# One layer-stack kernel, seven edits to its order: the start, the third output slabs, the last microseconds

## The reference

```
h = rmsnorm(x, g) * (1 + scale) + shift
x = x + gate * mixer(h)                     # layer 0: gated delta rule, 8 heads; layer 1: latent attention
h = rmsnorm(x, g') * (1 + scale') + shift'
x = x + gate' * swiglu(h)                   # width 2816
```

## Time and profile before

| | |
|---|---|
| median of three executions | 2261.05 us (2259.95 to 2262.13) |
| the profiled execution | 2260.28 us, its span 2258.4 us |
| busy: PE, DVE, ACT, POOL | 2163.2, 1168.5, 581.9, 1217.0 us |
| DMA | 240.40 MB, 106 GB/s over the span |

### The profile page before, as it was taken

The page is one execution under the profiler, slowest core; times in us unless marked ns, Lnnn a source line. Parts: engine busy times, 40 slices in busy tenths (PEclk is TensorE's granted clock), DMA queues, the critical chain, the costliest instruction groups (busy, mean ns, idle before and its releaser), DMA issues.

```text
span 2258.4 us, 29283 instructions
## 1 busy us (share of the span) xinstructions
PE 2163.2 (96%) x11996; PEld 1727.1 (76%) x11996; DVE 1168.5 (52%) x1634; ACT 581.9 (26%) x1054; POOL 1217.0 (54%) x688
## 2 busy tenths in 40 slices
PE   5999999899999999998999999999999999999997
PEld 4777777778888887676788888777767878887886
DVE  3566666657648275554431322467755365346332
ACT  4432433213102022342320201422332230002113
POOL 4532233347868776432566666654445276657663
PEclk9999999999999999999999999999999999999999
DMA  9422222226556463211433333322214133333331
GB/s 304 142 67 85 88 81 85 85 70 210 178 171 206 141 195 110 68 51 30 120 94 96 100 94 99 97 75 75 66 52 126 38 112 96 100 85 93 103 103 66
DMA packets 366016, 240.40 MB, mean 106 GB/s; under 512 B 11350, under 2 KB 350524, under 8 KB 365756
## 3 DMA queue, kind: packets, MB, share of 16 engines
q1 hardware_dynamic: 364268, 234.60, 34.5%
q10 hardware_dynamic: 1616, 3.93, 0.5%
HBM read 234.31 MB, written 4.19 MB: 106 GB/s over the span
## 4 chain that ended last, share of the span: by engine, by line
PE 88%; DVE 6%; POOL 2%; issue 2%; ACT 2%; DMA 1%; SPq 0%; ACTq 0%; DVEq 0%; POOLq 0%
PE bank L588 16%; PE bank L590 16%; PE bank L589 16%; PE bank L607 6%; PE bank L609 5%; PE bank L608 5%; PE mid L871 2%; PE mid L1333 1%; POOL wL L544 1%; PE bank L624 1%; DMA stage<-in_c_wkv 1%; PE bank L625 1%; PE bank L626 1%; PE mid L632 1%; PE bank L825 1%
## 5 line engine op out<-in xcount | busy, mean ns | idle before, releaser
L542 POOL TENSOR_SCALAR wH<-stage 128x1024 fp32r<-128x1024 f32 (+1 forms) x340 | 386.6, 1137 | 985.7 <-PE bank L609 375.1
L544 POOL TENSOR_TENSOR wL<-stage,wH 128x1024 fp32r<-128x1024 f32 (+1 forms) x340 | 830.3, 2442 | 28.4
L588 PE MATMUL bank<-hH,wH 128*128 128x512 f32 x944 | 368.7, 391 | 0.7 <-DVE A L2051 0.3
L590 PE MATMUL bank<-hH,wL 128*128 128x512 f32 x944 | 367.4, 389 | 0.0
L589 PE MATMUL bank<-hL,wH 128*128 128x512 f32 x944 | 367.3, 389 | 0.0
L588 PE MATMUL bank<-RA,wH 128*128 128x512 f32 (+1 forms) x788 | 285.8, 363 | 15.1 <-POOL wL L544 12.1
L590 PE MATMUL bank<-RA,wL 128*128 128x512 f32 (+1 forms) x788 | 282.7, 359 | 0.0
L589 PE MATMUL bank<-RA,wH 128*128 128x512 f32 (+1 forms) x788 | 282.7, 359 | 0.0
L607 PE MATMUL bank<-hH,wH 128*128 128x512 f32 x544 | 238.6, 439 | 0.3 <-DVE A L2051 0.3
L609 PE MATMUL bank<-hH,wL 128*128 128x512 f32 x544 | 213.5, 393 | 0.0
L608 PE MATMUL bank<-hL,wH 128*128 128x512 f32 x544 | 213.2, 392 | 0.0
(11 more groups left out here) (390 smaller groups left out, 3244.1 us busy)
## 6 DMA issues: line engine op xcount, KB each, us to landing
WIDE<-in_ada_t SPq DMA_DIRECT2D x48, 1024.0 KB, 6.1
stage<-in_ffn_w_gate SPq DMA_DIRECT2D x44, 512.0 KB, 3.9
stage<-in_ffn_w_up SPq DMA_DIRECT2D x44, 512.0 KB, 3.9
stage<-in_c_wkv SPq DMA_DIRECT2D x32, 512.0 KB, 3.9
stage<-in_gdn_w_in SPq DMA_DIRECT2D x32, 512.0 KB, 4.1
stage<-in_ffn_w_down SPq DMA_DIRECT2D x32, 512.0 KB, 3.8
stage<-in_o_w_in SPq DMA_DIRECT2D x32, 512.0 KB, 4.0
stage<-in_e_w_in SPq DMA_DIRECT2D x26, 512.0 KB, 3.8
```

The costliest lines, as they stand in the source:

```text
L542: pool.tensor_scalar(high[:, 0:n], raw[:, 0:n], 1.0, 0.0, ALU.mult, ALU.add).then_inc(w_high, 1)
L544: pool.tensor_tensor(low[:, 0:n], raw[:, 0:n], high[:, 0:n].bitcast(F32), ALU.subtract).then_inc(w_split, 1)
L588: pe.matmul(bank[:, 0:n], h[:, k, c], xh[:, k, :], start=first and k == 0, stop=False)
L590: mm = pe.matmul(bank[:, 0:n], l[:, k, c], xh[:, k, :], start=False, stop=last and k == kc - 1)
```

## The change

- **Start, loads.** x is loaded ahead of the memory; only the first two tables are loaded first, the rest and the column constants after the first two head slabs; kv slabs and groups alternate in SP's queue; a third slot holds groups; groups come in the order 0, 4, 1, 5, 2, 6, 3, 7, so that two of them complete two chunks' shift and scale; group 7 is loaded behind two head slabs; the small parameters come behind the seventh group.
- **Start, c.** c is loaded as one row by ACT's queue, and TensorE spreads it over the partitions with two multiplications by ones.
- **Start, x.** x is turned before the memory and copied by DVE instead of ACT. The memory turns have four banks instead of two.
- **Start, norm.** The norm is done two chunks at a time, in DVE's queue between the groups (`first_norm`), and in ACT's between the copies of kv slabs (`first_high`).
- **Gates.** The high and the low part of the 16 gate columns lie side by side, so two multiplications a chunk give all; the sums are added on DVE.
- **Third slabs divided.** Two to four thirds stand ahead of the last step, the others behind it, at all six places; in gdn five stand in the last head's later fillings and three behind.
- **End.** The squares' sums are taken in two halves, the last chunk's turned copy is DVE's, ACT's table is loaded ahead of the residual, and row blocks are sent in the order 2, 0, 3, 1.

```diff
+ADA_ORDER = (0, 4, 1, 5, 2, 6, 3, 7)
...
+        adaw.append(A[:, 12:16].rearrange("p (r a) t -> p r (a t)", r=ADA_ROWS))
...
+                slot = ada_use(n)[0]
+                if n >= 3:
+                    sp.wait_ge(ada_summed, n - 2 if n < ADA_HEAD else n - 1)
...
-            sp.dma_start(tab[:], a["square"]).then_inc(small_in, 16)
-            sp.dma_start(cols2[:], a["cols"]).then_inc(small_in, 16)
+            sp.dma_start(tab[:, 0:2 * P], a["square"][:, 0:2 * P]).then_inc(small_in, 16)
...
+            load_kv(2)
+            load_ada(1)
+            load_kv(3)
+            sp.wait_ge(m["mem"], 1)
             load_ada(2)
+            load_kv(4)
+            load_ada(3)
...
+            head_slabs(0, range(2))
+            load_ada(7)
+            sp.dma_start(tab[:, 2 * P:], a["square"][:, 2 * P:]).then_inc(tab_in, 16)
+            sp.dma_start(cols2[:], a["cols"]).then_inc(tab_in, 16)
+            head_slabs(0, range(2, 4))
...
-            for t in range(TT):
+            for t in (2, 0, 3, 1):
                 sp.wait_ge(scaled_out[t], 1)
...
+            pe.wait_ge(c_in, 17)
+            for n in range(2):
+                mm = pe.matmul(c_bank[:, n * T:(n + 1) * T], ones[0:1, :], cbc[0:1, n * T:(n + 1) * T], start=True, stop=True)
...
+            x_turn(range(KD))
+            for n in range(4):
+                memory(0, n)
             pe.wait_ge(x_memt, 8)
-            kv_slabs("m0", range(2))
...
+            kv_slabs("m0", (0,))
             norm_squares(range(4))
-            kv_slabs("m0", (4,))
+            kv_slabs("m0", (1,))
             norm_squares(range(4, KD))
-            kv_slabs("m0", range(5, 8))
+            kv_slabs("m0", range(2, 8))
...
-                pe.matmul(B3[:], h, hH[:, k, :], start=k == 0, stop=False)
-                pe.matmul(B3[:], h, hL[:, k, :], start=False, stop=False)
-                mm = pe.matmul(B3[:], l, hH[:, k, :], start=False, stop=k == KD - 1)
+                both = RA[:, 0, 32 * k:32 * k + P]
+                pe.matmul(B3[:], both, hH[:, k, :], start=k == 0, stop=False)
+                mm = pe.matmul(B3[:], both, hL[:, k, :], start=False, stop=k == KD - 1)
...
-                    fill(24 + t, 25 + t, third=(t,))
+                    fill(24 + t, 25 + t)
...
-                fill(28, 30, third=(4, 5))
+                fill(28, 30, third=(0, 1))
...
-                fill(30, 32, 6, third=(6,))
+                fill(30, 32, 6, third=(2, 3, 4))
...
-            out_third("gdn_out", 7, 7, 8)
+            for k in range(5, KD):
+                out_third("gdn_out", k, k, k + 1)
...
-            for k in range(2, 6):
-                out_third("mla_out", k, k, 8 + k + 1)
+            out_third("mla_out", 2, 2, 8 + 3)
             for k in (6, 7):
                 out_step("mla_out", k, k, 8 + k + 1)
-            for k in (6, 7):
+            for k in range(3, KD):
                 out_third("mla_out", k, k, 8 + k + 1)
...
-            for n in range(7):
+            for n in range(4):
                 e_out(n, out_third)
             e_out(7)
-            e_out(7, out_third)
+            for n in range(4, KD):
+                e_out(n, out_third)
...
-                for k in range(6):
+                for k in range(2):
                     out_third(f"x{r}_out", k, k, 24 + 16 * r + k + 1)
...
-                for k in (6, 7):
+                for k in range(2, KD):
                     out_third(f"x{r}_out", k, k, 24 + 16 * r + k + 1)
...
-            for k in range(KD - 1):
+            for k in range(2):
                 out_third("o_out", k, k, 32 + k + 1)
             out_step("o_out", KD - 1, KD - 1, 32 + KD)
-            out_third("o_out", KD - 1, KD - 1, 32 + KD)
+            for k in range(2, KD):
+                out_third("o_out", k, k, 32 + k + 1)
...
+            early_copies((0,))
             squares_of_x(range(4))
+            early_copies((1,))
             squares_of_x(range(4, KD))
+            inv_sqrt(ss_done, SS0[1], SS, SS[:], 1.0 / D, load=False).then_inc(rstd_ready, 1)
+            early_copies(range(2, 5))
+            first_high(range(2))
             early_copies((5,))
-            rstd_of(RUN_OF["mix0"], SS)
-            early_copies((6, 7))
-            early_spill(1)
-            norm("mix0", modT[:, 0:8], load=False)
+            first_high(range(2, 4))
+            early_copies((6,))
+            first_high(range(4, 6))
+            early_copies((7,))
+            first_high(range(6, KD))
...
+            def first_norm(pair):
+
+                ks = range(2 * pair, 2 * pair + 2)
+                cols = slice(2 * pair, 2 * pair + 2)
+                dve.wait_ge(ada_summed, 2 * pair + 2)
+                own(dve.scalar_tensor_tensor(out=gainA[:, 0, cols], in0=modT[:, 8 + 2 * pair:10 + 2 * pair], scalar=1.0,
+                                             in1=col["mix0"][:, cols], op0=ALU.add, op1=ALU.mult))
+                own.settle()
+                for k in ks:
...
+            for n in range(4):
+                ada_sum(n)
+            dve.wait_ge(x_ready, KD)
+            dve.wait_ge(rstd_ready, 1)
+            for pair in range(2):
+                first_norm(pair)
+            for pair in range(2, 4):
+                for n in range(2 * pair, 2 * pair + 2):
+                    ada_sum(n)
+                first_norm(pair)
```

More of the change, by code:

```diff
@@ L288, in build @@
         taken = [sem(f"taken{n}") for n in range(2)]
-        ada_loaded = [sem(f"ada_loaded{n}") for n in range(2)]
+        ada_loaded = [sem(f"ada_loaded{n}") for n in range(3)]
         ada_summed, c_in = sem("ada_summed"), sem("c_in")
+        tab_in = sem("tab_in")
         small_in, x_in, vec_in, par_in, wide_in, mem_in = (
@@ L725, in _ @@
             pe.wait_ge(vec_ready, 1)
-            for n in range(4):
-                memory(0, n)
+            pe.wait_ge(c_in, 17)
+            for n in range(2):
+                mm = pe.matmul(c_bank[:, n * T:(n + 1) * T], ones[0:1, :], cbc[0:1, n * T:(n + 1) * T], start=True, stop=True)
+            mm.then_inc(m["c"], 1)
             xtok = A[:, 0:8].rearrange("p (t a) c -> p t (a c)", t=TT)
@@ L1497, in memory_rows @@
                     own.settle()
-                own(inv_sqrt(act_own, own.now(), mss[:, 2:4], mss[:, 0:2], 1.0 / D))
+                own(inv_sqrt(act_own, own.now(), mss[:, 2:4], mss[:, 0:2], 1.0 / D, load=r == 1))
                 own.settle()
@@ L2120, in _ @@
             dve.tensor_copy(vec[:, 0:VEC_ROWS], B3[:, 0:VEC_ROWS]).then_inc(vec_ready, 1)
-            dve.wait_ge(m["c"], 1)
-            dve.wait_ge(vec_ready, 1)
-            own(dve.memset(gate_row.bitcast(F32), 0.0))
-            dve.wait_ge(small_in, 32)
+            for k in range(KD):
+                dve.wait_ge(turned, k + 2)
+                dve.tensor_copy(xT[:, k, :], x_banks[k % 2]).then_inc(x_ready, 1)
+            dve.wait_ge(vec_ready, 1)
+            for n in range(4):
+                memory_low(0, n)
@@ new lines, in _ @@
+            own(dve.memset(gate_row.bitcast(F32), 0.0))
+            dve.wait_ge(m["c"], 1)
+            def first_norm(pair):
[5 more added lines that the diff above has]
+                own.settle()
+                for k in ks:
+                    if pair:
+                        dve.wait_ge(h_ready, k - 1)
+                    dve.scalar_tensor_tensor(out=(B4, B7)[k % 2][:], in0=xT[:, k, :], scalar=gainA[:, 0, k:k + 1], in1=SS,
+                                             op0=ALU.mult, op1=ALU.mult).then_inc(t_ready, 1)
+                for k in ks:
+                    dve.wait_ge(hh_ready, k + 1)
+                    dve.scalar_tensor_tensor(out=hL[:, k, :], in0=(B4, B7)[k % 2][:], scalar=modT[:, k:k + 1],
+                                             in1=hH[:, k, :].bitcast(F32), op0=ALU.add, op1=ALU.subtract).then_inc(h_ready, 1)
@@ L2125, in _ @@
+            for n in range(4):
+                ada_sum(n)
[7 more added lines that the diff above has]
+                first_norm(pair)
+            dve.wait_ge(tab_in, 32)
             unit = table("ident64")[0:64]
             dve.tensor_tensor(pick[0:64, :], unit[:, 0:8], unit[:, 32:40], ALU.add).then_inc(g["pick"], 1)
-            ada_sum(0)
@@ L2128, in _ @@
-            for n in range(4):
-                memory_low(0, n)
-            for n in range(1, ADA_HEAD):
-                ada_sum(n)
-            gain_of(0, col["mix0"], 8)
-            dve.wait_ge(x_ready, KD)
-            norm("mix0", gainA[:, 0], modT[:, 0:8])
+            own(dve.tensor_copy(cbc[:], c_bank))
+            dve.wait_ge(h_ready, KD)
             pads = A[:, 14:18].rearrange("p a c -> p (a c)")[:, 0:3 * 516].rearrange("p (n c) -> p n c", n=3)
```

172 lines of the change are left out of this document (88 added, 84 removed).

## The result

The changed kernel takes 2232.82 us (median of four, 2231.63 to 2234.73), the kernel before 2260.50 (four, 2259.64 to 2262.13): a ratio of 0.9876, interval 0.9864 to 0.9888. The span fell from 2258.4 to 2231.0, 27.4 us, where 15.3 were forecast. The direction and most of the single terms were right; one term was much too small and two places were missing from the sum.

What follows compares the result with a forecast made beforehand. TensorE was taken as the bound (88% of the span). Start 1.5, thirds 12.4 and tail 1.4 sum to 15.3 us: 2260.28 - 15.3 = 2245.0, for the median 2245.7; range 2238 to 2252.

Steps and rivals of the forecast that it cites:

- The thirds: Dividing third slabs at six places fills TensorE's waits for GpSimd's split: 12.4 us, of which gdn 1.5.
- The start: The stretch up to TensorE's end of the first eight chunks: 3.9 us earlier, less 2.4 for slow clock, 1.5 us.
- x and the memory land: Loads at the start: memory lands some 2 us later, at 14.2, with bytes priced at 404 GB/s.
- product 0: First weight product on TensorE at the start: 5.5 us, from 24.9 to 30.4.
- the gain that GpSimd blocked: VectorE's gains in the first norm: one of them held up under GpSimd's subtraction, 1.7 us.
- The last low part: End of VectorE's chain in the first norm: 75.9, with TensorE through the eight chunks at 77.1.
- the start is warm: Rival, chance 0.25: turns and c's row bring 2.4 GHz, product 0 takes 2.9, up to 3.7 us earlier, 2242.0.
- the idle time ahead of chunk 6: At the start TensorE waits for chunks and idles about 5 us before chunk 6.
- cost there what they cost here: Small packets of the convolution weights move behind group 6 in the DMA queue, at unchanged cost.
- The loss to the clock: After idling at the start, TensorE's multiplications run at 1.2 GHz, 0.43 apart instead of 0.23: 2.4 us lost.
- The tail: End of the kernel: table load moved ahead and row blocks reordered, first output DMA 1.4 us earlier.

Runs made afterwards that it cites:

- e1: The kernel before with only the six divisions of the third slabs added; 2248.76 us, ratio 0.9942.
- e10: Changed kernel with early high parts, small loads behind two head slabs, and the last head's four-column copy on ScalarE instead of VectorE; 2230.76 us.
- e3: The changed kernel with the thirds of gdn alone put back as before; 2234.48 us, ratio 0.9881.
- e9: The changed kernel with c loaded into all partitions and its silu copied by ScalarE, as before, instead of multiplications by ones; 2235.00 us.
- e8: The changed kernel with 24 unused turns of the identity on TensorE in the hole ahead of the first weight product; 2233.43 us.
- e5: The kernel before with one added wait: GpSimd splits the first gdn_out slab only after VectorE's fourth instruction of the last head; 2257.55 us, ratio 0.9984.

## Why the prediction was wrong, step by step

- **The thirds: right.** Sum 12.4, measured 13.0 alone in e1. The spacing in the earlier trace rows and the hole plus clock in the earlier trace rows carried over to four other places within 0.3 us. In gdn it was 1.7 with the old start (e1) and 1.3 to 1.6 with the new one where the clock held (e10 against e3); in the changed kernel the clock, fallen behind a wait of 1.87, took it back.
- **The start: the failed step, "the start brings 3.9 - 2.4 = 1.5 us"; it brought 5.5 to 7.8.** Three terms of the sum were mis-sized, all the same way: x and the memory land 1.8 us earlier than reckoned (I priced all bytes at 404 GB/s; c's load, which no longer stands ahead of x, had cost 2.4 us and not 1.3 (e9), and the other 0.7 stays open); product 0 took 4.4 and not 5.5, because the turns had brought the clock up (e8, e9); the gain that GpSimd blocked lost 0.7 and not the 1.7 that I took. The last low part came at 70.2 instead of 75.9. These three make 3.9 of the 5.7 us; of the others, 0.7 lies between the scaled memory and product 0, where the memory turns ran at full pace, and 1.0 in the rest of VectorE's chain. The rival "the start is warm", held at 0.25, had the right mechanism, and product 0 gained 1.1 of the 2.6 us that it gave; against it I had held that turns don't lift the clock, which e9 refutes.
- **A wait missed.** The prediction put the idle time ahead of chunk 6. It stood ahead of chunk 0, since the head slab's load had moved behind the small packets. I counted what those cost ("cost there what they cost here") and not who stands behind them in SP's queue. So VectorE's chain ended 5.7 us earlier than forecast, but the chunks only 2.4 (74.7 against 77.1). The loss to the clock is in the 74.7 already (eleven multiplications at 0.43 instead of 0.23, 2.2 us), where the prediction took 2.4 off once more: 2.4 + 2.4 are the 4.8 of the table. That the loss to the clock had nearly the forecast size is luck: it fell behind another hole than the one it was reckoned for.
- **The last head: missing from the sum.** I saw the copy of 2.35 in the earlier trace rows and used it only as a price for the gains at the start. It and its neighbour each waited for one of GpSimd's subtractions; one such wait less gave 3.1 us and what the clock adds, and it hangs on half a microsecond of a transfer.
- **The start of latent attention: missing too.** It gave 0.7 us, and 1.5 more where the clock held behind the hole of 1.81. Which of the two comes is chance, so 1.5 of the 27.4 us are luck of the profiled execution.
- **The tail: right** (1.4, measured 1.2 to 1.4).
- **The range** was made of the terms that I had, so it held no room for a place that only shifts in time.

## What to carry to other kernels

Where an engine is held up under another's work, or a hole is just long enough to lose the clock, a shift of half a microsecond far ahead can be worth several: look for such places before summing an edit, and widen the range by them. When a load moves in a queue, ask who stands behind it, not only what it costs. And when two constraints end together, test both edits at once: each alone was worth nothing here, both likely some 2 us. Before a place of two traces is compared, compare its granted clock: it hid the whole gain of the gdn thirds.

## What the runs showed of the hardware that was not expected

- Turns alone brought TensorE to the 2.4 GHz level: 0.12 us between multiplications of 256 columns right behind them in e9, 0.21 once the clock had fallen for a hole of 2.96 us.
- A hole of 1.81 us lost the clock in six of eleven executions, one of 2.54 us did not in the kernel before and did in e1 and e5, and one of 2.19 at the start of e10 did not: at such lengths no row tells beforehand which, and it is worth 1.5 to 2.6 us. (Ahead of the first output step of gdn the waits of 1.38 to 1.72 us kept it in four profiles, those of 1.86 to 2.04 lost it in ten; but one of 1.57 behind it lost it in e5.)
- A subtraction of 128x256 on VectorE took 2.59, 1.25 or 0.42 us as it started 0.09 us behind GpSimd's subtraction, 0.06 behind GpSimd's first pass (the rounding), or 0.20 ahead of that; a copy of four columns took 2.35, 1.03 or 0.16.
